# A hybrid decoder layer on one core: six units of the query and key projection ahead of the first scores instead of five and a half

## The reference

```python
q = apply_rope(q.reshape(B, T, ATT_HEADS, 2, ATT_HEAD_DIM), pos)
k = apply_rope(k.reshape(B, T, ATT_HEADS, 2, ATT_HEAD_DIM), pos)
...
s = jnp.einsum("bqhmd,bkhmd->bhmqk", qblk, k).astype(f32) * scale
s = jnp.where(causal, s, jnp.float32(-1e30))
p = jax.nn.softmax(s, axis=-1)
w = p[:, :, 0] - lam * p[:, :, 1]
return jnp.einsum("bhqk,bkhe->bqhe", w.astype(v.dtype), v)
```

## Time and profile before

| | |
|---|---|
| median of 3 runs | 1152.84 us (1152.07 to 1156.08) |
| the profiled execution's own time | 1152.76 us |
| its span in the trace | 1151.0 us |
| PE busy | 1122.8 us (98%) |
| DVE busy | 785.3 us (68%) |
| ACT busy | 399.2 us (35%) |
| POOL busy | 52.7 us (5%) |
| the chain that ended last | PE 89%, DVE 5%, DMA 2%, ACT 1%, issue 1% |

### The profile page before, as it was taken

One profiled execution on the slowest core, in us unless ns is written; L12 is line 12 of the kernel. 1 busy time (PEld: TensorE's weight loads), 2 busy tenths in 40 slices (PEclk: granted clock), 3 DMA queues, 4 the chain that ended last, 5 costly groups with the idle time before them and its releaser, 6 DMA issues.

```text
span 1151.0 us, 14008 instructions
## 1 busy us (share of the span) xinstructions
PE 1122.8 (98%) x5110; PEld 908.4 (79%) x5110; DVE 785.3 (68%) x1127; ACT 399.2 (35%) x728; POOL 52.7 (5%) x94
## 2 busy tenths in 40 slices
PE   7999999999989999999999999999999999999996
PEld 6888887777756788878888888888888888888885
DVE  6666765756577546888867667766766666766768
ACT  7433933545567326642212112212221211211222
POOL 0300001000121110000000000000000000000010
PEclk9999999999999999999999999999999999999998
DMA  6111323111010456111121011110211102111062
GB/s 229 56 37 36 136 84 89 58 37 38 21 35 19 148 182 200 73 37 74 37 73 36 36 73 36 45 64 36 73 36 41 69 36 73 36 36 73 37 234 113
DMA packets 23397, 83.11 MB, mean 72 GB/s; under 512 B 3088, under 2 KB 3216, under 8 KB 23232
## 3 DMA queue, kind: packets, MB, share of 16 engines
q1 hardware_dynamic: 17424, 62.92, 15.3%
q0 software_dynamic: 5648, 19.60, 5.0%
q10 hardware_dynamic: 288, 0.09, 0.0%
HBM read 70.02 MB, written 8.39 MB: 68 GB/s over the span
## 4 chain that ended last, share of the span: by engine, by line
PE 89%; DVE 5%; DMA 2%; ACT 1%; issue 1%; SPq 0%; POOL 0%; DVEq 0%; ACTq 0%
PE pair L352 27%; PE pair L354 27%; PE pair L353 27%; PE pair L725 3%; PE pair L760 2%; DMA raw<-weights 2%; PE pair L742 1%; PE pair L728 1%; DVE y_gain L2087 1%; PE pair L574 1%; DVE yacc L2072 1%; DMA q_rot<-q_sb 1%; DVE h_sb L2101 1%; DVE negmax L1657 0%; DVE wl L1478 0%
## 5 line engine op out<-in xcount | busy, mean ns | idle before, releaser
L354 PE MATMUL pair<-wdh,xl 128*128 128x512 f32 x480 | 186.7, 389 | 0.0
L352 PE MATMUL pair<-wdh,xh 128*128 128x512 f32 x480 | 186.7, 389 | 0.0
L353 PE MATMUL pair<-wdl,xh 128*128 128x512 f32 x480 | 186.7, 389 | 0.0
L1883 DVE TENSOR_TENSOR yacc<-yacc,pair 128x1024 f32<-128x1024 f32 x104 | 127.0, 1221 | 80.2 <-PE pair L354 80.2
L1378 ACT ACTIVATE up_h<-raw 128x384 fp32r<-128x384 f32 x56 | 27.4, 513 | 226.9 <-DMA raw<-weights 226.9
L353 PEld LDWEIGHTS pair<-wdl,xh 128*128 128x128 f32 x480 | 90.1, 188 | 18.7
L352 PEld LDWEIGHTS pair<-wdh,xh 128*128 128x128 f32 x480 | 90.1, 188 | 18.7
L354 PEld LDWEIGHTS pair<-wdh,xl 128*128 128x128 f32 x480 | 90.1, 188 | 18.7
L352 PE MATMUL pair<-xh,wh 128*128 128x512 f32 x256 | 102.2, 399 | 1.0 <-DVE xl L1501 1.0
L354 PE MATMUL pair<-xh,wl 128*128 128x512 f32 x256 | 99.9, 390 | 0.0
L353 PE MATMUL pair<-xl,wh 128*128 128x512 f32 x256 | 99.7, 389 | 0.0
(11 more groups left out here) (305 smaller groups left out, 2099.1 us busy)
## 6 DMA issues: line engine op xcount, KB each, us to landing
raw<-weights SPq DMA_DIRECT2D x74, 512.0 KB, 3.3
wd_f<-weights SPq DMA_DIRECT2D x28, 512.0 KB, 3.6
x_sb<-x SPq DMA_DIRECT2D x8, 512.0 KB, 7.7
q_rot<-q_sb POOLq DMA_DIRECT2D x32, 128.0 KB, 2.7
out<-h_sb POOLq DMA_DIRECT2D x8, 512.0 KB, 3.5
h_sb<-out POOLq DMA_DIRECT2D x8, 512.0 KB, 11.2
out<-h_sb SPq DMA_DIRECT2D x7, 512.0 KB, 2.6
x_a<-x POOLq DMA_DIRECT2D x4, 512.0 KB, 6.8
```

The source lines that it names most:

```text
L352: pe.matmul(o, a_hi, b_hi, start=first, stop=False)
L353: pe.matmul(o, a_hi, b_lo, start=False, stop=False)
L354: return pe.matmul(o, a_lo, b_hi, start=False, stop=last)
L1883: dve.tensor_tensor(y, y, pair[2 + t % 2][:, :], ALU.add).then_inc(y_added, 1)
```

## The change

The projection ahead of the first scores grows from five and a half units to six, and ACT copies six units there. The other ten units fill steps 1 to 20 and are due in the even steps 2, 4, ..., 20. All that follows `unit_end` moves one step forward.

```diff
         def unit_end(u):
 
-            return 2 * (u - EARLY) + 1 if u > EARLY else 1
+            return 2 * (u - EARLY)
...
-            project(KC * EARLY + KC // 2)
+            project(KC * EARLY + KC)
             pe.wait_ge(const_ready, 1)
             pe.wait_ge(act_step, 1)
...
-            for u in range(EARLY):
+            for u in range(EARLY + 1):
                 unit_copy(u)
...
                 if s >= 1:
                     wt_copy_step(s - 1)
-                for u in range(EARLY, UNITS):
+                for u in range(EARLY + 1, UNITS):
                     if unit_end(u) == s:
                         unit_copy(u)
```

## The result

The changed kernel takes 1165.6 us in the median of 4 runs (1162.52 to 1165.92), the kernel before 1153.26 in the runs beside it (1152.07 to 1156.08). The ratio is 1.0097 with a 95% interval of 1.0075 to 1.0118: slower. (The means of these runs give that ratio too; the two medians alone would give 1.0107.) The profiled execution took 1162.52 us, the fastest of the four, with a span of 1160.7; it is 9.8 us above the profiled one of before, the forecast was 9.1. The other three are 3 us higher still, and the median lies 1.1 us above the end of the range, 1164.5.

A forecast was written before the change was run, and what follows sets the result against it. PE, busy for 98% of the span, bounds the kernel, so work or waiting added there counts. 0.9 + 4.4 + 2.7 + 1.1 = 9.1 us on 1152.76 us gives 1161.9 us; range 1157.6 to 1164.5.

The forecast's parts named there:

- Front: Up to step 5's scores: the half unit fills PE's idle time but the first exponential comes later; +0.9 us.
- Unit copies: Steps 5 to 21: ACT copies units late in even steps, so PE waits in odd ones; +4.4 us (3.6 to 5.6).
- Transfers in steps 5 to 17: POOL's transfers and the cosine shift with the copies, but PE's filler hides the delay; 0 us.
- Step 21: PE waits for head variances behind DVE's cosine, +3.5 us; step 23 returns 0.8 as its maxima lose the sine ahead.
- Clock: Step 21: PE's long wait drops the granted clock to half for the work behind it; +1.1 us (0 to 2.5).
- the one with the clock up in step 21: Rival: step 21 blocks PE, but the clock does not fall; +8.0 us, 1160.8 us; chance 0.18.
- the one with the transfers in time: Rival: copies cost as forecast, but transfers land before DVE needs them; +6.2 us, 1159.0 us; chance 0.10.
- The faster one: Rival: the waits before step 0 and head 3's scores go, no new one comes; -3.7 us, 1149.1 us; chance 0.03.
- that of no change: Rival: filled idle time before step 0 and small new waits leave it within 2 us, about 1153.5 us; chance 0.07.
- The table load's price: Rival: at the first exponential, the load holds ACT for a second 1.28 us; +10.4 us, 1163.2 us; chance 0.04.
- The two old waits: PE's waits before step 0 (1.97 us) and ahead of head 3's first scores (1.74 us), both forecast to go.

The follow-up runs named there:

- front edit: Changed kernel with a one-element exponential ahead of unit 5's copy, and the high part and DVE's work on piece 2 moved later; 1164.21 us, profiled execution only.
- copies-first edit: Changed kernel with ACT copying each unit right behind the exponentials, ahead of output copy, square and transposed weights; 1155.28 us, ratio 1.0012 to the kernel before.
- the second experiment: Changed kernel with the last piece's cosine, sine and sum back in steps 22, 23 and 23; 1160.37 us, ratio 1.0052 to the kernel before.
- the busy PE: Changed kernel plus 20 unused matmuls ahead of the sums of squares in PE's step 21; 1162.58 us, ratio 1.0079 to the kernel before.
- the control: Changed kernel without any edit, profiled a second time; 1164.19 us, ratio 1.0095 to the kernel before.
- the corrected versions: Changed kernel with relieved front, unit copies first and last cosine back in step 22, without or with step 21's variances ahead of the maxima; 1150.57 and 1150.46 us.
- the last one: Changed kernel with relieved front, unit copies first, last cosine back in step 22, and step 21's variances right behind the combination; 1150.46 us, ratio 0.9973.
- the variances first: Changed kernel with step 21's head variances ahead of the last piece's cosine, behind the maxima; 1161.18 us, ratio 1.0071 to the kernel before.
- all three: Changed kernel with relieved front, unit copies first, and the last piece's rope work back in steps 22 and 23; 1150.57 us, ratio 0.9978 to the kernel before.

## Why the prediction was right, and where its sizes were off

- **Front, forecast +0.9:** +0.94 at the mark of step 5, by the mechanism that was named, at the times that were named (exponential 195.97 for 195.95, transposes 202.38 for 202.5). The front edit undoes it, down to 0.14.
- **Unit copies, forecast +4.4:** the marks of steps 5 and 21 are 5.26 us further apart in the profiled execution, 5.1 of it by this term and 0.1 by the next. The waits themselves are 1.48 and 1.47 us in steps 9 and 17, for 1.55; the rest is PE's start behind a wait, about 0.2 us each time: 1.69 us between the marks for 1.55, 0.34 for 0.2 and 0.47 for 0.4; step 7 adds 0.12 for 0.05 and step 15 nothing. The term's upper end (5.6) had counted that start and was the better guess. That ACT's order makes all of it is shown by the copies-first edit.
- **Transfers in steps 5 to 17, forecast 0:** this is the sentence that failed. I took 5.3 us from copy to cosine everywhere, from a row at the end of the filler. The kernel before had longer ones where DVE waited for the transfers, 5.97 and 6.21 us for the first two pieces ahead of step 0. In step 13 it is 6.0 in the profile after and 7.2 in that of the second experiment, and then 0.1 to 1.3 us reach PE in step 15, up to 1.4 in step 7 (the front edit's profile).
- **Step 21, forecast +3.5 and -0.8 behind it:** PE went on 8.41 us after the scores (8.6), which makes +3.3 at full clock; between the marks of steps 23 and 24 it is -0.81. The wait for `hvar` is 5.91 us. The cosine's place explains it: with the cosine back, 6.7 us go, 2.7 of them the clock's.
- **Clock, forecast +1.1:** the net is +1.2, but of other parts. The fall in step 21 costs 1.4 us until the scores and 1.3 in them, 2.7 together, which the busy PE gave back; and the fall of the kernel before in step 24 did not come (1.09 us for the same eight transposes), which returned 1.5. I had priced the first too low and had not thought of the second.
- **What was missing:** a fall of the clock in step 9, behind the new wait there. It costs 1.6 us and came in three of the six profiles that have this wait (the control, the cosine back, the busy PE). Why in these three stays open. With the late transfers it accounts for the 2 to 3 us in which the other executions exceed the profiled one, and for the median beyond the range. For executions without a profile that is an inference from those with one.
- **Rivals:** the one with the clock up in step 21 is excluded by the windows, and the one with the transfers in time by the cosine's wait of 2.86 us there. The faster one and that of no change are excluded by the `q_sb` waits and the 9.8 us; the condition of the faster one, ACT's copy done before PE leaves the scores, is what the copies-first edit makes true. The table load's price is as in its row: the exponential starts 1.30 us after the load's start, which excludes a second stretch of that length. The Trainium skill's page "ScalarE: Activation LUTs", section "What ACT_TABLE_LOAD costs", puts a drain of about 1.38 us beside the load. This trace shows none, and the measurement decides.
- **The two old waits:** both are gone in the changed kernel, but neither gave its time back. The one before step 0 is filled with the half unit in the corrected versions too; the one ahead of step 24 is there again with 1.29 us. What these versions gain (0.2 to 0.3%) lies in step 21: without filler it takes 4.99 us in the last one, in place of 6.74.

## What to carry to other kernels

When a hand-ordered schedule moves by one step, look at what each engine does in the new step ahead of the moved work: steps of different parity, or one step with something special, have another order. Follow a wait through the queue behind it, as an operation that waits for a transfer holds back small ones for which another engine waits. And price a new wait on TensorE with the clock that it can cost, in every place where one appears, not in the longest alone.

## What the runs showed of the hardware

- TensorE's granted clock fell to 0.50 (1.2 of 2.4 GHz) behind a wait of only 1.48 us, in three of six profiles that have this wait in step 9; the steps just ahead (marks 8 to 9) were as long in all six, 5.76 to 5.77 us. It cost 1.6 us. The wait of 1.47 us in step 17 brought it down in none of the six. A wait of 1.75 to 1.83 us in step 21 did so in two profiles (the variances first, all three) and not in a third (the cosine back). The idle 1.97 us before step 0 did not bring it down: the granted clock was 1.00 there.
- Four transfers of 128 KB from SBUF to SBUF took from 5.2 us (the cosine of step 21 after the change) to 7.3 us (the front edit, step 5) between the start of the copy that releases them and that of the operation that waits for them. With the issues at the same distances it was 6.26 us in one execution and 7.22 in another.
- Twenty matmuls put into a wait of 5.9 us kept the granted clock at 1.00 and made the stretch around it 2.7 us shorter.
